# Retention's decays as products of two one-sided decays, made ahead by ScalarE and GpSimd; group norm's roots spread beside attention's values

## The reference

```python
def retention_chunkwise(q, k, v, lg, s0):
    ...
    dmask = jnp.where(diff >= 0, jnp.exp(lgc[:, :, None] * jnp.maximum(diff, 0.0)), 0.0)
    s = jnp.einsum('bhncd,bhnmd->bhncm', qc, kc) * dmask[None, :, None]
    o_intra = jnp.einsum('bhncm,bhnme->bhnce', s, vc)
    ...

def retention_bidir(q, k, v, lg_f, lg_b, s_f, s_b):
    o_f, fin_f = retention_chunkwise(q, k, v, lg_f, s_f)
    o_b, fin_b = retention_chunkwise(jnp.flip(q, 2), jnp.flip(k, 2), jnp.flip(v, 2), lg_b, s_b)
    return o_f + jnp.flip(o_b, 2), fin_f, fin_b

def retention_out(o, g):
    ...
    var = jnp.mean(jnp.square(of - mu), axis=-1, keepdims=True)
    on = ((of - mu) * lax.rsqrt(var + EPS)).astype(o.dtype)
    return merge_heads(on) * jax.nn.silu(g)
```

## Time and profile before

| | us |
|---|---|
| runs of the kernel before: median of 3 (lowest, highest) | 1813.71 (1813.0, 1814.03) |
| the profiled execution's own time | 1811.02 |
| its span on the core | 1809.2 |
| TensorE busy in the span | 1727.3 (95%) |
| VectorE, ScalarE, GpSimd busy | 1075.1, 732.9, 205.5 |

### The profile page before, as it was taken

How to read it: one execution, slowest core, us unless ns; L and a number is a source line. 1 busy time by engine, 2 the same in 40 slices (tenths; PEclk the granted TensorE clock), 3 DMA queues, 4 the chain that set the end, 5 groups by cost and what they waited for, 6 DMA issues and landing times.

```text
span 1809.2 us, 27271 instructions
## 1 busy us (share of the span) xinstructions
PE 1727.3 (95%) x11108; PEld 1541.9 (85%) x11108; DVE 1075.1 (59%) x1717; ACT 732.9 (41%) x1236; POOL 205.5 (11%) x204
## 2 busy tenths in 40 slices
PE   5899988889999999999999999999999999999997
PEld 3899862679999999999999984333999999999997
DVE  2777647783756787785475845657474653333345
ACT  2422324473664312213344664564465432221332
POOL 2000000342100000000120032343310000000012
PEclk8899999999999999999999999999999999999998
DMA  9355221112446456564411210000333642222221
GB/s 335 103 177 164 87 64 35 30 50 69 128 130 196 129 154 184 153 180 116 118 39 36 85 30 1 1 1 24 94 107 105 204 116 76 70 82 70 81 84 59
DMA packets 255279, 179.47 MB, mean 99 GB/s; under 512 B 12862, under 2 KB 228787, under 8 KB 254131
## 3 DMA queue, kind: packets, MB, share of 16 engines
q1 hardware_dynamic: 255154, 177.72, 33.0%
HBM read 174.15 MB, written 3.62 MB: 98 GB/s over the span
## 4 chain that ended last, share of the span: by engine, by line
PE 85%; DVE 7%; issue 3%; ACT 2%; POOL 1%; DMA 1%; SPq 0%; POOLq 0%; ACTq 0%; DVEq 0%
PE ps L747 22%; PE ps L749 22%; PE ps L748 22%; PE ps L1288 3%; PE ps L1298 2%; PE ps L784 1%; PE ps L889 1%; PE ps L891 1%; PE ps L890 1%; PE ps L1197 1%; PE ps L794 1%; DVE w_lo L546 1%; POOL rstd L2536 1%; DVE pA L2215 1%; PE ps L780 1%
## 5 line engine op out<-in xcount | busy, mean ns | idle before, releaser
L537 ACT ACTIVATE w_hi<-stage 128x1024 fp32r<-128x1024 f32 (+1 forms) x178 | 186.6, 1050 | 640.8 <-PE ps L749 534.3
L546 DVE TENSOR_TENSOR w_lo<-stage,w_hi 128x1024 fp32r<-128x1024 f32 (+1 forms) x178 | 220.8, 1242 | 295.0 <-ACT w_hi L537 294.7
L747 PE MATMUL ps<-hM_hi,w_lo 128*128 128x320 f32 x952 | 295.5, 310 | 0.0
L749 PE MATMUL ps<-hM_hi,w_hi 128*128 128x320 f32 x952 | 294.4, 309 | 0.0
L748 PE MATMUL ps<-hM_lo,w_hi 128*128 128x320 f32 x952 | 294.4, 309 | 0.0
L747 PE MATMUL ps<-h_hi,w_lo 128*128 128x320 f32 x824 | 256.1, 311 | 2.6 <-DVE h_lo L2322 2.6
L749 PE MATMUL ps<-h_hi,w_hi 128*128 128x320 f32 x824 | 254.8, 309 | 0.0
L748 PE MATMUL ps<-h_lo,w_hi 128*128 128x320 f32 x824 | 254.8, 309 | 0.0
L2536 POOL TENSOR_TENSOR rstd<-rstd,sq 128x320 f32<-128x320 f32 x75 | 77.4, 1038 | 999.3 <-ACT sq L1377 996.7
L747 PEld LDWEIGHTS ps<-hM_hi,w_lo 128*128 128x128 f32 x952 | 178.8, 188 | 3.4 <-issue 3.4
L748 PEld LDWEIGHTS ps<-hM_lo,w_hi 128*128 128x128 f32 x952 | 178.8, 188 | 0.0
(11 more groups left out here) (381 smaller groups left out, 3535.7 us busy)
## 6 DMA issues: line engine op xcount, KB each, us to landing
stage<-in_w_mlp_out SPq DMA_DIRECT2D x83, 512.0 KB, 4.2
stage<-in_w_mlp_in SPq DMA_DIRECT2D x80, 512.0 KB, 4.4
slab_mlp<-in_w_ada SPq DMA_DIRECT2D x28, 1024.0 KB, 5.3
stage<-in_w_in_ac SPq DMA_DIRECT2D x28, 512.0 KB, 3.8
slab_ac<-in_w_ada SPq DMA_DIRECT2D x12, 1024.0 KB, 6.1
ada_a<-in_w_ada SPq DMA_DIRECT2D x8, 1024.0 KB, 17.4
stage<-in_w_out_ac SPq DMA_DIRECT2D x8, 512.0 KB, 4.1
stage<-in_w_out_c SPq DMA_DIRECT2D x8, 512.0 KB, 4.1
```

The lines of the kernel that those rows point to most:

```text
L537: nc.scalar.activation(hi_place(n)[:, 0:width], stage[:, n % STAGE, 0:width], ACT.Copy)\
L546: nc.vector.tensor_tensor(lo_place(n)[:, 0:width], stage[:, n % STAGE, 0:width], hi_place(n)[:, 0:width].bitcast(F32), ALU.subtract).then_ ...
L747: mm(out, lo[:, k], xh, start=j == 0, stop=False)
L749: last = mm(out, hi[:, k], xh, start=False, stop=j == k_tiles - 1)
```

## The change

- A decay of heads 3 to 7 is no longer the smaller of two exponentials, but a product of two one-sided ones: exp(lg x max(d, 0)) and exp(-lg x min(d, 0)). Two new `tensor_scalar` on VectorE split the distance once (`dpos`, and `dist` in place). GpSimd makes the product and adds the diagonal (`decay_product`). Heads 0, 1 and 2 keep VectorE's minimum and stand ahead of the retention; head 2's second exponential goes to `sq`.
- The states are loaded ahead of the two first pieces of `out0`, on a semaphore of their own, and centred before the retention. The mask is loaded behind the last exponential.
- VectorE's split of piece 25 moves from between the second and third centring to behind the fifth. ScalarE copies `nv`'s second bank first.
- In a pair's order on TensorE, the context stands before the third values for every pair, and the transposes of keys stand in pairs 1 and 2 instead of behind them. On ScalarE the first head of the next pair goes ahead of a pair's copies, the second behind them.
- Group norm's squares are summed per 128 tokens (20 calls instead of 24). The roots are spread in `na_values` of steps 1 to 7, three blocks a step, into the free columns of the values' bank, and multiplied in `na_store`. `gn_spread` and `normed` are gone. ScalarE's high halves of the four retention pairs move from steps 4, 6, 8, 10 to 8, 9, 11, 13.

The core of the diff:

```diff
@@ DVE
+                dve.wait_ge(d_used, 2 * m + 2)
                 dve.wait_ge(rs_done, NB * m + kt + 1)
...
                 centred(rv[:, b, :], src, vmean[:, b, :]).then_inc(v_out, 1)
-                if b == 1:
-                    dve_split(dve, 25)
+            dve_split(dve, 25)
             dve.wait_ge(decay_exp, 3)
             smaller_decay(0)
             dve_split(dve, 26)
             smaller_decay(1)
             dve_split(dve, 27)
+            smaller_decay(2)
+            dve.wait_ge(state_in, 16 * 4)
+            flat = state[:].rearrange("p m s d -> p (m s d)")
+            centred(flat, flat, smean[:]).then_inc(state_done, 1)
             dve.wait_ge(v_done, 8)
+            ts(dpos[:], dist[:], 0.0, None, ALU.max).then_inc(d_sides, 1)
+            dve.wait_ge(d_sides, 1)
+            ts(dist[:], dist[:], 0.0, None, ALU.min).then_inc(d_sides, 1)
...
@@ POOL
-            pool.wait_ge(ret_out, PAIRS)
+            def decay_product(h):
+
+                pool.wait_ge(d_exp, h + 1)
+                sub(two(dmat[:, h % 4, :]), two(dmat[:, h % 4, :]), back_place(h), ALU.mult).then_inc(d_prod, 1)
+                pool.wait_ge(d_prod, h - 2)
+                diagonal = two(dmat[:, h % 4, :])[:, :, 384:512]
+                sub(diagonal, diagonal, ident[:, None, :].to_broadcast([P, 2, P]), ALU.add).then_inc(d_used, 1)
+
+            for h in range(3, 2 * PAIRS):
+                decay_product(h)
+            pool.wait_ge(qe_done, PAIRS)
             nc.gpsimd.memset(bm[:, :, :, NKEY:NKEY + NP], 0.0).then_inc(bias_zero, 1)
@@ ACT
+            head_decays(2)
             act.wait_ge(v_done, 8)
-            for b in range(5):
+            for b in (1, 0, 2, 3, 4):
                 f(nv[:, b, :], ps[:, V_BANKS[b], :], ACT.Copy).then_inc(v_out, 1)
-            act.wait_ge(ret_in, 16 * 5)
+            head_decays(3)
+            act.wait_ge(ret_in, 16)
             query_decays(0)
...
+            query_decays(1)
+            for m in range(1, PAIRS):
                 if m < PAIRS - 1:
                     head_decays(2 * m + 2)
+                ret_copy(m - 1)
+                if m < PAIRS - 1:
                     head_decays(2 * m + 3)
+                    if m == 1:
+                        past_copy()
+                    else:
+                        new_copy()
                     query_decays(m + 1)
...
-            high_at = {4: 0, 6: 1, 8: 2, 10: 3, 12: 4, 17: 5, 21: 6}
+            high_at = {8: 0, 9: 1, 11: 2, 13: 3, 14: 4, 17: 5, 21: 6}
@@ PE, na_values, and DVE, na_store
+                for n, (pair_m, block) in enumerate(gn_blocks(t)):
+                    for e in range(2):
+                        root = gnr[:, 5 * pair_m + block, e:e + 1].to_broadcast([P, HD])
+                        last = mm(ps[64 * e:64 * e + 64, 6 + t % 2, P * (n + 1):P * (n + 2)], root, ident[:],
+                                  start=True, stop=True)
                 last.then_inc(na_pv, 1)
...
+                pairs = [p for p, _ in gn_blocks(t)]
+                for p in sorted(set(pairs)):
...
+                    last = tt(oT[:, p, tokens], oT[:, p, tokens], ps[:, 6 + t % 2, P * (n + 1):P * (n + 1 + count)], ALU.mult)
```

More of the change, by code:

```diff
@@ L343, in build @@
         rpb_rows = nc.dram_tensor("rpb_rows", (NH, ROWS, ROWS * RPB_C), F32).ap()
+        [dpos] = lay(105, ("dpos", [P, 1024], F32))
         [dback] = lay(128, ("dback", [P, 1024], F32))
@@ L576, in back_place, with gn_blocks @@
         def back_place(h):
-            return two(dback[:]) if h >= 2 else sq[:, :, 0:512]
+            return two(dback[:]) if h >= 3 else sq[:, :, 0:512]
+        def gn_blocks(t):
+            return [divmod(n, 5) for n in range(3 * (t - 1), 3 * t) if 0 <= n < 5 * PAIRS]
         block = top.enter_context(nc.Block())
@@ L653, in _ @@
                         n += 1
+            sp.wait_ge(ada_acc, OPS * G_AC)
+            for s, name in enumerate(("state_ret_fwd", "state_ret_bwd")):
+                for e in range(2):
+                    sp.dma_start(state[64 * e:64 * e + 64, :, s, :],
+                                 i[name][0, 0].rearrange("(m e) k v -> e k m v", e=2)[e]).then_inc(state_in, 16)
             for j in range(2):
@@ L669, in _ @@
                              rpb_rows[:].rearrange("h r x -> r h x")).then_inc(na_bias_in, 16)
-            sp.dma_start(mask[:], i["c_mask"]).then_inc(na_in, 16)
             sp.wait_ge(v_out, 10)
@@ L673, in _ @@
                          nv[:, NB, :].rearrange("p (h d) -> p h d", h=NH)).then_inc(stored, 16)
+            sp.wait_ge(d_exp, 2 * PAIRS)
+            sp.dma_start(mask[:], i["c_mask"]).then_inc(na_in, 16)
             sp.wait_ge(nk_out, 1)
@@ L942, in ret_end, with past_turned, new_turned @@
                 last.then_inc(ret_done, 1)
+            def past_turned():
+                pe.wait_ge(past_in, 16 * 2)
+                pe.wait_ge(ret_out, 1)
+                for j in range(4):
+                    last = nc.tensor.transpose(ps[:, 4, P * j:P * (j + 1)],
+                                               kpast[:, 2 * j:2 * j + 2, :].rearrange("p h d -> p (h d)"), ident[:])
+                last.then_inc(past_t, 1)
+            def new_turned():
+                pe.wait_ge(ret_out, 2)
+                for j in range(4):
+                    last = nc.tensor.transpose(ps[:, 5, P * j:P * (j + 1)], kn[:, j, TL:T], ident[:])
+                last.then_inc(nk_t, 1)
             pe.wait_ge(mod_out, ADA_START + G_AC // 2)
             ret_scores(0, 0)
-            pe.wait_ge(v_out, 7)
+            pe.wait_ge(v_out, 6)
             ret_scores(0, 1)
-            pe.wait_ge(v_out, 10)
-            ret_context(0)
             for m in range(PAIRS):
+                if m == 0:
+                    pe.wait_ge(v_out, 7)
                 if m >= 2:
@@ L965, in _ @@
                 ret_end(m)
-                if m == 1:
-                    pe.wait_ge(past_in, 16 * 2)
-                    pe.wait_ge(ret_out, 1)
-                    for j in range(4):
-                        last = nc.tensor.transpose(ps[:, 4, P * j:P * (j + 1)],
-                                                   kpast[:, 2 * j:2 * j + 2, :].rearrange("p h d -> p (h d)"), ident[:])
-                    last.then_inc(past_t, 1)
-                if m == 2:
-                    pe.wait_ge(ret_out, 2)
-                    for j in range(4):
-                        last = nc.tensor.transpose(ps[:, 5, P * j:P * (j + 1)], kn[:, j, TL:T], ident[:])
-                    last.then_inc(nk_t, 1)
             def na_scores(t):
@@ L1052, in _ @@
             na_scores(1)
-            gn_sums()
             for m in range(PAIRS):
-                gn_spread(m)
-            pe.wait_ge(gn_done, PAIRS)
+                gn_sums(m)
+            pe.wait_ge(ret_out, PAIRS)
             pe.wait_ge(nvs_done, 1)
@@ L1495, in head_decays @@
                     act.wait_ge(qe_done, (h - 4) // 2 + 1)
-                if h:
+                if h >= 4:
+                    act.wait_ge(d_prod, h - 3)
+                elif h == 3:
+                    act.wait_ge(d_sides, 2)
+                elif h:
                     act.wait_ge(d_used, h)
-                f(dmat[:, h % 4, :], dist[:], ACT.Exp, scale=out_lg[:, h:h + 1])
+                f(dmat[:, h % 4, :], dpos[:] if h >= 3 else dist[:], ACT.Exp, scale=out_lg[:, h:h + 1])
                 f(back_place(h), two(dist[:]), ACT.Exp, scale=back_lg[:, h:h + 1]).then_inc(d_exp, 1)
@@ L2219, in na_store @@
                 dve.wait_ge(na_pv, t + 1)
+                pairs = [p for p, _ in gn_blocks(t)]
+                for p in sorted(set(pairs)):
+                    n, count = pairs.index(p), pairs.count(p)
+                    first = gn_blocks(t)[n][1]
+                    tokens = slice(P * first, P * (first + count))
+                    dve.wait_ge(gn_gated, p + 1)
+                    last = tt(oT[:, p, tokens], oT[:, p, tokens], ps[:, 6 + t % 2, P * (n + 1):P * (n + 1 + count)], ALU.mult)
+                    if first + count == 5:
+                        last.then_inc(gn_done, 1)
                 nc.vector.tensor_copy(oT[:, 4 + m, P * b:P * (b + 1)], ps[:, 6 + t % 2, 0:P]).then_inc(na_out, 1)
@@ L2225, in _ @@
             gn_inverse()
-            for m in range(PAIRS):
-                normed(m)
             for t in range(1, N_NA + 4):
```

82 lines of the change are left out of this document (30 added, 52 removed).

## The result

The changed kernel took 1797.2 us (median of 4 runs, 1794.85 to 1799.24) against 1813.87 us for the kernel before on the same chip (1813.0 to 1814.03): a ratio of 0.9909, 95% interval 0.9891 to 0.9926. It was faster, and the forecast, 1796.2 us, lies 1 us under the median. The profiled execution was the slowest of the four: 1799.24 us, span 1797.3. So its 11.8 us against the profile of before (1811.02) are less than the medians' 16.7: 2.0 of the difference lie between this execution and its median, 2.9 between that of before and its own. A good part of what follows is about what makes executions of one kernel differ.

The account below looks back on a forecast made before the run. TensorE was taken to bound the kernel (85% of the chain), with gains only where it idles or is clocked low. 2.5 + 14.0 + 7.0 - 4.0 - 0.5 - 1.5 = 17.5 us gave 1796.2 us, range 1793 to 1800.

Parts of the forecast that it names:

- A: Value projection: with the weight split behind the fifth centring, TensorE no longer waits for centred `rv`; gain 2.5 us.
- B: Retention: decays made ahead and products on GpSimd let TensorE pace the pairs; 63.4 us become 49.4, gain 14.0 us.
- C: Group norm's stretch before attention's loop: fewer sums and no spread in front; 16.1 us become 9.1, gain 7.0 us.
- D: Attention's loop pays: -4.0 us for roots and multiplications, -0.5 for its start, -1.5 for the low clock.
- I take 1.4 us for both: Retention's start: the two new clamps of 1024 columns, priced at 1.4 us together although GpSimd fills `bias` then.
- Twice that beside GpSimd: Retention's start: by the skill's two read ports, both clamps take 1.1 us alone and twice that beside GpSimd.
- Rival 2: Retention: GpSimd's products, at 5.5 us each, pace the pairs; two pairs wait 2.5 us each; 1801.2 us, chance 0.08.
- Rival 1: Attention's loop pays more, -11 instead of -6 us, both engines being near full; 1801.2 us, chance 0.14.
- rival 4: Attention's loop: the clock stays down at 1.2 GHz, so the kernel is slower, 1835 us; chance 0.03.
- Rival 3: Attention's loop: its added work fits the slack (-2.5 us) and the clock is up at once; 1792 us, chance 0.08.
- the other signs that I named: Among them: 9 to 10 us from last retention matmul to first softmax factor; wrong if a later stage changes length.
- Whatever is gained moves the rest as a block: From the output projection on nothing edited remains, so earlier gains shift the rest of the program unchanged.

Follow-up runs that it names:

- first profile: The profiled execution of the changed kernel in its first measurement against the kernel before: 1799.24 us, span 1797.3; the median there was 1797.2 us.
- first repetition: The changed kernel run again without an edit, against the kernel before on the same chip: median 1794.99 us, ratio 0.9882.

## Why the prediction was right, and where its terms were off

Gains in us, each stage read from the profiles:

| step | forecast | first profile | first repetition |
|---|---|---|---|
| ahead of 228 us | 0 | 0.55 | -0.39 |
| A, value projection | 2.5 | 2.5 | 2.5 |
| B, retention | 14.0 | 10.7 | 12.3 |
| C, group norm | 7.0 | 5.6 | 7.7 |
| D, loop | -6.0 | -4.1 | -5.2 |
| tail | 0 | -3.4 | -0.4 |
| span | 17.5 | 11.9 | 16.5 |

That the total came within 1 us of the median is in part luck. In the first repetition B's missing 1.7 us is nearly made up by 0.7 in C and 0.8 in D; in the profiled execution of the first comparison the stages fall 5.6 us short.

**A** came out to the tenth. TensorE no longer waits for `rv`, and putting the split back brings back the 1.28 us wait and 2.5 us in all.

**B** had the right mechanism and one term mis-sized. Pairs 1 and 2 took 12.16 us each (12.25 forecast), pair 3 10.47 (10.3), pair 0 11.58 at full clock (11.65). The step that failed is "I take 1.4 us for both, near the undisturbed row since a fill reads nothing". Alone the two clamps take 1.39 us, as said; beside the fill they took 3.18. The reason I gave was the wrong one: a clamp is not slowed in proportion, it is kept out for as long as the fill runs (1.92 us, and 0.70 + 1.92 is 2.62, of which 2.49 are seen). The Trainium skill (SBUF — State Buffer, Who interferes with whom) says this of a VectorE instruction in a two-port mode: who is first gets the shared pair for the whole instruction, and the other fully blocks. The rows agree that the clamp is blocked; who was first they don't tell, since the clamp's row begins 0.03 us ahead of the fill's. By that rule an estimate of the term is 3.3 us. "Twice that beside GpSimd", which my prediction had made of the two read ports, is not what the rows show: the whole cost fell on the clamp beside the fill, and the other took 0.69. The fill was in my text, and its duration in the row of the POOL engine; adding that 1.92 us would have put B at 12.1.

GpSimd's product was 2.36 us (2.7 forecast) and its slack held: in the first repetition the last diagonal for the third pair ended at 282.48 us, and VectorE began the scores that need it at 283.69. Rival 2 fell in its first half, that GpSimd paces the pairs. Its last sentence, "the products were only moved, and the gain is TensorE's order and the group norm", is borne out for the products, though not under its condition: the products on VectorE gave the same time.

**C** is within 1.4 us of both profiles. My 5.2 us for the sums lies between 4.6 and 6.8, and which of them comes is decided by when the clock falls, which differs between executions of one kernel.

**D** was put too high: 4.1 and 5.2 us against 6.0, and about 1.1 of the 5.2 is the longer fall at the late hole, of which I said nothing. The roots cost about 3.5 us, forecast 4.0, with the quantities as said (80 records and nine multiplications of 4.0 us). Start and clock together cost 0.6, forecast 2.0: the clock is low over the loop's first steps as I said (0.60 and 0.72 granted from 315 to 325 us in the first repetition), but TensorE has idle time there to lose (busy 3.18 of the 5.00 us from 315 to 320). Rival 1 (-11) and rival 4 (the clock stays down) both fell: the granted clock of the loop was 0.92. The Trainium skill's sentence on transposes (TensorE: Matmul & The Clock Gate, Part 4), on which rival 4 leaned, is not borne out in this loop: in the first profile the granted clock was back at 1.00 from 330 to 335 us, with its third of transposes, and stayed there up to the late hole. The fall to 0.50 behind that hole is what I had named as a sign of being wrong; the kernel before does it too. Rival 3 was half right: the start and the clock came cheap, the roots did not.

C and D together, the group norm's part alone, were mis-sized most. Their net was 1.0 us by my terms, and 3.65 by the run with the old group norm, whose loop loses the same 3.4 us of clock at the late hole as the repetition's that it is held against. Of the 2.65 us between them 0.6 is C's (16.13 us became 8.52) and 2.0 is D's (57.56 became 61.52, so 4.0 was paid for the roots and the start, and not 6.0). A forecast of the group norm's part alone would have been wrong by more than twice its size.

Of the other signs that I named, two came by the clock: the stretch from the last retention matmul to the first softmax factor was 10.66 and 8.52 us instead of 9 to 10, and the tail changed its length.

**"Whatever is gained moves the rest as a block"** is true to about 3 us between profiles of the changed kernel and no better. The tail was 1412.7 to 1419.1 us in the twelve profiles, all with the same instructions in it. The forecast's range held this, but for no reason that I gave.

## What to carry to other kernels

When an instruction is added beside one of GpSimd's, look for what GpSimd does in that very moment, a plain fill included, and add its whole duration; then ask whether the fill could stand anywhere else. Before work is given to GpSimd, ask whether VectorE was short of time or only of its inputs: here it waited for inputs, and GpSimd's part in the change was worth nothing. And compare stages between events in two profiles of one kernel before explaining a difference of 2 or 3 us in a whole of 1800.

## What the runs showed of the hardware

- A VectorE clamp of 1024 fp32 columns took 2.49 us beside a GpSimd fill of 1.92 us, and 0.70 without it. An instruction with two SBUF inputs was slower beside GpSimd's product (query products 2.00 us for two, against 1.28), but it stayed at 1.28 where it overlapped with the moved fill. Score products, which read PSUM, took 1.29 us for two beside GpSimd's product too.
- 1024 columns with two inputs: GpSimd 2.36 us, VectorE 1.22.
- A string of two-column matmuls ran at 0.112 us each, until the clock fell within it or just behind it, in each of the profiles read here. Put in another place, it took the fall along.
- Hundreds of us later, where TensorE hardly waits, every fall of the granted clock in 660 us began within a string of one-column matmuls or at most 1.3 us behind it: at a string of 24 records in eleven profiles of twelve, at one of 18 to 20 in 6 cases of 120. With the falls farther on, (1 - granted clock) x time comes to 13.6 to 18.8 us of a tail of 1413 to 1419.
- VectorE's low half of a weight piece in the loop took 2.37 us, against 1.23 in the value projection, and TensorE then waited 2.54 us, in the kernel before as with the change.
